# Which DMA queue carries the early weight units of a decoder layer, and behind what

## What is computed

```
mod = silu(c) @ w_ada + b_ada                      # w_ada: 2048 x 12288
sh1, sc1, g1, sh2, sc2, g2 = split(mod, 6)
h = rms_norm(x, norm1_w) * (1 + sc1) + sh1         # the first norm
proj = h @ w_in                                    # w_in: 2048 x 7168
y = [dilated attention(proj), gated recurrence(proj)] @ w_out
x = x + g1 * y
h = rms_norm(x, norm2_w) * (1 + sc2) + sh2
x = x + g2 * (gated conv FFN(h))                   # w_up, w_down
out = rms_norm(x, final_norm_w)
```

## Time and profile before

| | |
|---|---|
| median of three runs | 1294.17 us |
| the profiled execution | 1293.13 us, its span 1291.3 us |
| busy share of the span | PE 97%, PE weight loads 86%, DVE 77%, ACT 48%, POOL 4% |
| early stage | about the first 145 us of the span |
| DMA in slices of 32.3 us, from the start | 338, 386, 386, 349, 272 GB/s |

### The profile page before, as it was taken

How to read it: one execution, slowest core, us unless ns; L and a number is a source line. 1 busy time by engine, 2 the same in 40 slices (tenths; PEclk the granted TensorE clock), 3 DMA queues, 4 the chain that set the end, 5 groups by cost and what they waited for, 6 DMA issues and landing times.

```text
span 1291.3 us, 20752 instructions
## 1 busy us (share of the span) xinstructions
PE 1254.3 (97%) x7190; PEld 1106.8 (86%) x7190; DVE 991.0 (77%) x1286; ACT 619.1 (48%) x884; POOL 50.3 (4%) x98
## 2 busy tenths in 40 slices
PE   5899899999999999999999999999999999999997
PEld 5888899998988888888888888888888888888886
DVE  4788799999998889788788788879677766545454
ACT  3335565555656645554444444444444444434342
POOL 0000100031130000000000000000000000000000
PEclk9789899999999999999999999999999999999999
DMA  9999788888798899667777777777666676555553
GB/s 338 386 386 349 272 310 276 279 283 293 244 322 288 296 357 370 241 245 245 244 229 237 232 237 233 231 241 218 191 192 183 191 268 215 191 193 193 194 195 115
DMA packets 155988, 329.44 MB, mean 255 GB/s; under 512 B 11493, under 2 KB 20438, under 8 KB 155026
## 3 DMA queue, kind: packets, MB, share of 16 engines
q1 hardware_dynamic: 152352, 318.49, 74.1%
q0 software_dynamic: 3280, 9.66, 2.2%
q10 hardware_dynamic: 290, 0.44, 0.1%
HBM read 322.77 MB, written 4.19 MB: 253 GB/s over the span
## 4 chain that ended last, share of the span: by engine, by line
PE 89%; DMA 4%; DVE 3%; issue 2%; ACT 1%; SPq 1%; DVEq 0%; ACTq 0%
PE bank L1296 25%; PE bank L1304 13%; PE bank L1360 6%; PE bank L1361 6%; PE bank L1359 6%; PE bank L1041 5%; PE bank L1043 5%; PE bank L1042 5%; PE bank L1028 4%; PE bank L1030 4%; PE bank L1031 4%; DMA pc<-in_w_ada 3%; DVE acc_c L1455 2%; DMA wraw<-in_w_out 1%; PE bank L998 1%
## 5 line engine op out<-in xcount | busy, mean ns | idle before, releaser
L681 ACT ACTIVATE whi<-wraw 128x1024 fp32r<-128x1024 f32 x408 | 424.8, 1059 | 576.6 <-PE bank L1304 239.2
L1443 DVE TENSOR_TENSOR wlo<-wraw,whi 128x1024 fp32r<-128x1024 f32 x403 | 489.9, 1221 | 243.2 <-ACT whi L681 242.0
L1296 PE MATMUL bank<-h,whi 128*128 128x512 f32 x1400 | 334.3, 391 | 0.2 <-DVE h L1728 0.2
L1296 PEld LDWEIGHTS bank<-h,whi 128*128 128x128 f32 x1400 | 257.2, 188 | 50.4 <-issue 0.6
L1304 PEld LDWEIGHTS bank<-h,wlo 128*128 128x128 f32 x1400 | 179.6, 191 | 6.9
L1304 PE MATMUL bank<-h,wlo 128*128 128x256 f32 x1400 | 181.7, 283 | 0.0
L1028 PE MATMUL bank<-h,whi 128*128 128x256 f32 x512 | 148.7, 290 | 5.2 <-DVE h L1468 5.2
L1030 PE MATMUL bank<-h,whi 128*128 128x256 f32 x512 | 145.7, 285 | 0.0
L1031 PE MATMUL bank<-h,wlo 128*128 128x256 f32 x512 | 145.7, 285 | 0.0
L1359 PE MATMUL bank<-whi,act_hi 128*128 128x512 f32 x336 | 130.8, 389 | 0.0
L1360 PE MATMUL bank<-wlo,act_hi 128*128 128x512 f32 x336 | 130.8, 389 | 0.0
(11 more groups left out here) (250 smaller groups left out, 1328.3 us busy)
## 6 DMA issues: line engine op xcount, KB each, us to landing
wraw<-in_w_up SPq DMA_DIRECT2D x176, 512.0 KB, 3.8
araw<-in_w_ada SPq DMA_DIRECT2D x128, 512.0 KB, 5.3
wraw<-in_w_in SPq DMA_DIRECT2D x112, 512.0 KB, 4.9
wraw<-in_w_down SPq DMA_DIRECT2D x88, 512.0 KB, 3.7
pc<-in_w_ada SPq DMA_DIRECT2D x48, 512.0 KB, 11.5
wraw<-in_w_out SPq DMA_DIRECT2D x32, 512.0 KB, 6.3
pc<-in_w_ada SPq DMA_DIRECT2D x32, 256.0 KB, 6.8
x<-in_x SPq DMA_DIRECT2D x2, 1024.0 KB, 7.8
```

The lines of the kernel that those rows point to most:

```text
L681: act.activation(whi[:, slot], wraw[:, slot], ACT.Copy).then_inc(s_hi, 1)
L1296: pe.matmul(ps[bank0 + f], whi[:, (ph.unit0 + j) % RING, k, f * P:(f + 1) * P], h[:, kk].rearrange("p a t -> p (a t)"), start=(kk == 0), s ...
L1443: dve.tensor_tensor(wlo[:, slot], wraw[:, slot], whi[:, slot].bitcast(F32), ALU.subtract).then_inc(s_lo, 1)
```

## The change

SP no longer loads the units 4 to 24; after units 0 to 3 its stream holds pieces only, up to the 80th. ACT issues the loads of units 4 to 24 on its own queue: `load_early(v)` waits until the low part of unit v - 4 is done, as SP did, and then issues the same DMA. In ACT's stream it stands behind a high part: after the high part of unit v comes the load of unit v + 3, and after the second unit of a chunk also that of v + 4, ahead of `chunk_hi`. `LOADS_AT` is gone. The orders of PE, DVE and POOL are unchanged.

```diff
-LOADS_AT = ((3, 7, 11, 15, 15, 15), (3, 7, 11, 15, 15, 15), (3, 7, 11, 15, 15, 15), (5, 10, 15))
 ...
             for m in range(CHUNKS - 1):
-                v = U0[m] + RING
                 for r in range(KT):
                     load_first((m + 1) * KT + r)
-                    for _ in range(LOADS_AT[m].count(r)):
-                        load_in(v)
-                        v += 1
 ...
+            def load_early(v):
+
+                act.wait_ge(s_lo, v - RING + 1)
+                n, j = unit_of(v)
+                name, g = GROUPS[n]
+                col = COLUMN[name] + g * UW
+                src = w_in[j * UK * P:(j + 1) * UK * P, col:col + UW].rearrange("(k p) n -> p k n", p=P)
+                act.dma_start(wraw[:, v % RING], src).then_inc(s_w[v % RING], 16)
+
+            u = RING
             for v in range(LATER):
                 first_hi(v)
+                while u < U0[-2] + RING and u < v + RING + (v - 1 in U0):
+                    load_early(u)
+                    u += 1
                 for n in range(CHUNKS):
                     if v == U0[n] + 1:
                         chunk_hi(n)
```

## The result

The changed kernel took 1297.61 us in the median (1296.14 to 1298.51, 20 runs), the kernel before on the same chip 1294.28 (1292.77 to 1296.49, 20 runs). The ratio is 1.0023 [1.0017, 1.0029]: slower by 3.3 us. The forecast was 1298.3, with a range of 1294.6 to 1302.0. Like for like, the profiled execution took 1296.42 us against 1293.13; its span grew by 3.2 us. So the sign was right and the size was 0.8 us too large. The parts of the sum show where those 0.8 us went.

The account below looks back on a forecast made before the run. It took full DMA engines to bound the early stage, chunk 2's last piece setting a fixed stretch. Terms 0 + 4.06 + 0 = 4.1 us on 1294.17 gave 1298.3 us; own range 1296.9 to 1299.1, overall 1294.6 to 1302.0.

Parts of the forecast that it names:

- A unit on ACT's queue passes SP's backlog: Early stage: queues take turns packet by packet, so units land 4 to 7 us after issue instead of 11.4.
- Three units pass in chunk 1, the piece lands at 69.8: Chunk 1: units 7, 8 and 9 go ahead of the last piece, landing at 69.8 us instead of 65.7.
- A1 of chunk 1 follows by the same 4.1 us: DVE in chunk 1: A1, done at 70.16 us before, follows the last piece, which moves from 65.7 to 69.8 us.
- Three units pass in chunk 2, the piece lands at 99.5, A1 of chunk 2 ends 4.06 us later: Chunk 2: three more units ahead move the last piece from 95.4 to 99.5 us, A1 from 99.95 to 104.0.
- The last piece sets A1 of chunk 2: DVE in chunk 2: A1 follows the landing of the last piece, 4.55 us later.
- DVE would wait more for pieces in chunk 2: Sign in the profile: DVE waits for pieces in chunks 1 and 2 more than before; no size given.
- From A1 of chunk 2 on the length is fixed: From A1 of chunk 2 to the early stage's end: the distance stays at 40 us, shifted by the same 4.06 us.
- ACT's 21 issues cost nothing; mixing two queues costs nothing: ACT and DMA, early stage: issues at 0.44 us counted as 0; two-queue sharing, at most 0.8 us, also as 0.
- PE has some 4 us more of idle time before 145 us: Sign in the profile: PE's idle time before 145 us grows by some 4 us.
- the order of issue holds: DMA rival: transfers served in issue order whatever the queue, so 0 to 1.36 us, say 1294.9 us; chance 0.16.
- The units fall behind: Rival: ACT issues loads later, units come behind last pieces, A1 of chunk 2 up to 2.7 us earlier, 1291.5 us; chance 0.10.
- slow issues: ACT rival: 2.57 us per issue adds 3.6 us at two exposed places, 1301.9 us; chance 0.12.

Follow-up runs that it names:

- The experiments with one passing each: Two edits of the changed kernel: units pass the last pieces of chunk 1 only, 1297.86 us, or of chunk 2 only, 1297.58 us.
- the kernel with nine units still on ACT's queue: Against the changed kernel, units 7 to 9, 10, 11, 13 to 15, 19 to 21 and 24 back on SP's queue; 1294.46 us, ratio 1.0001.
- the first experiment: Against the changed kernel, units 7 to 9, 13 to 15, 19 to 21 and 24 back on SP's queue behind the pieces; 1296.48 us, ratio 1.0014.
- the experiment with chunk 2 alone: Against the changed kernel, units 7 to 9, 19 to 21 and 24 behind the pieces, 13 to 15 on ACT's queue; 1297.58 us, ratio 1.0022.

## Why the prediction came out as it did

- *A unit on ACT's queue passes SP's backlog.* Right. Units took 3.8 to 9.2 us from issue to landing, 7.2 in the median; the forecast was 4 to 7, a little too short.
- *Three units pass in chunk 1, the piece lands at 69.8.* Right, to 0.1 us (69.7).
- *A1 of chunk 1 follows by the same 4.1 us.* It came 5.0 us later. Left out was what the wait does to PE: the sum after 3.15 us of idle time took 3.57 us at 0.50 of the clock, not 1.98, of which 0.9 us came through to A1.
- *Three units pass in chunk 2, the piece lands at 99.5, A1 of chunk 2 ends 4.06 us later.* This is the term of the sum that was mis-sized: 2.8 us for the piece, 2.99 for A1. The low part of unit 11, which unit 15 waits for, was taken to be some 2 us later; it ended at 96.0 instead of 92.2, 3.8 later. So unit 15 went out too late to pass, and the 4.06 us of the sum became 3.0 at A1 of chunk 2 and 3.2 at the end of the span.
- *The last piece sets A1 of chunk 2.* Only half right. In the changed kernel the two arms meet: 98.2 + 4.55 = 102.75 by the piece, 75.13 + 27.8 = 102.9 by DVE's order, and 102.94 was measured. That DVE would wait more for pieces in chunk 2 was therefore wrong: it had no such wait, where the other arm decided. The experiments with one passing each show both arms. That the arms end within 0.2 us of each other is luck: the forecast was added up from the piece alone, and in the changed kernel DVE's order decided.
- *From A1 of chunk 2 on the length is fixed.* Right, to 0.01 us.
- *ACT's 21 issues cost nothing; mixing two queues costs nothing.* Right: 0.37 to 0.46 us an issue, 387 GB/s, and 1.0001 in the kernel with nine units still on ACT's queue.
- *PE has some 4 us more of idle time before 145 us.* It has 5.2 more (busy 113.38 us instead of 118.56), but 3.1 of them lie ahead of A1 of chunk 0, which isn't late. From 44.3 us to A1 of chunk 4 its waits went from 11.1 to 13.2 us, 2.1 more, and its busy time from 87.84 to 88.74 us for the same 618 matmuls, 0.9 more, at a granted clock of 0.90 instead of 0.91. Together these are the 3.0 us.

Of the rivals, "the order of issue holds" asked for 0 to 1.36 us and units that pass nothing. "The units fall behind" asked for a faster kernel, "slow issues" for rows of 2.57 us on ACT. None of them is in the trace. Two statements of the Trainium skill's page "DMA: Bandwidth & Descriptors" bear on this. That engines go round the queues that have work (section "Queues, rings and completion order"), the trace agrees with, by the landing of 7.2 us against 13.2. By the sentence that another issuer saves only the time of the issue (section "Issuing engines are not separate DMA queues"), taken alone, the change would have been worth nothing; the measured 3.3 us decide against reading it so.

## What to carry to other kernels

When the DMA engines are full, a second queue adds no bandwidth but changes who is served first: before moving loads to it, count the bytes that will now stand ahead of the transfer someone waits for, and leave loads that nobody waits for behind it. An early load that only removes the waits of an engine off the path (30 us of ACT's here) is worth nothing and can cost what it passes. Where two chains meet at one point, work out both: removing or delaying one shows only as far as the other lets it.

## What the runs showed of the hardware

- ACT issued its 21 loads in 373 to 463 ns each while SP's issues, behind their own backlog, took up to 5278 ns. So SP's backlog didn't slow the issue on ACT's queue. Line 718 of the changed kernel (issue time in ns min/median/max), then line 498:

```profile
L718 ACTq DMA_DIRECT2D wraw<-in_w_in x21: 373/374/463, 38.4 to 132.9; - x21
...
DMA to landing us min/median/max: 3.8/7.2/9.2
```

```profile
L498 SPq DMA_DIRECT2D pc<-in_w_ada x80: 367/1212/5278, 2.6 to 132.0; - x80
```

- Half of the engines would carry a unit in 2 x 1.355 = 2.7 us, but the median landing is 7.2. A unit on the emptier queue thus takes longer than an even share by this estimate; whether it is served late or slowly, that is what the other 4.5 us are, was not tried.
- A wait of PE can cost more than its own length. Behind 3.15 us of idle time in the changed kernel and 2.69 in the first experiment PE worked at 0.50, and 16 matmuls took 3.57 and 3.58 us. At the sum of chunk 1 the kernel before needed 1.98, and behind 2.79 us of idle time in the experiment with chunk 2 alone the same 16 of a piece took 1.95, and the granted clock from 85 to 92 us was 0.76. What decides between the two isn't shown by these runs.
